# Stage ends by token tile, and five down projections per expert layer in fp32, in a one-core transformer kernel

## What is computed

```python
u = modulate(rmsnorm(h, g_norm_ffn1), sh1, sc1)
h = h + 0.5 * gt1 * swiglu(u, w_ffn1_in, w_ffn1_out)          # "ffn1"
u = modulate(rmsnorm(h, g_norm_mix), sh2, sc2)
h = h + gt2 * token_mixing(u, ...)                            # "mix", ends in @ w_out
u = modulate(rmsnorm(h, g_norm_ffn2), sh3, sc3)
h = h + 0.5 * gt3 * swiglu(u, w_ffn2_in, w_ffn2_out)          # "ffn2"
x = rmsnorm(h, g_final)
for l in range(2):
    ret_o, swa_o, mla_o = ...                                 # from x @ w_in[l]
    mix = concatenate([ret_o, swa_o, mla_o], -1) @ w_out[l]   # "OUT"
    x = layer_norm(ALPHA * x + mix, ln1_g[l], ln1_b[l])
    # 16 experts, 2 per token: h = x @ w_gate_up[e]; a = silu(h[:256]) * h[256:] * gate
    #                          y += a @ w_down[e]
    x = layer_norm(ALPHA * x + grouped_moe(x, ...), ln2_g[l], ln2_b[l])
```

## Time and profile before

| | us |
|---|---|
| time of three runs, median (lowest to highest) | 1220.62 (1219.76 to 1225.07) |
| profiled execution, its own time | 1219.01 |
| its span in the trace | 1217.2 |
| PE, DVE, ACT busy | 1102.7, 898.8, 638.4 |
| read from HBM | 269.41 MB |

### The profile page before, as it was taken

How to read it: one execution, slowest core, us unless ns; L and a number is a source line. 1 busy time by engine, 2 the same in 40 slices (tenths; PEclk the granted TensorE clock), 3 DMA queues, 4 the chain that set the end, 5 groups by cost and what they waited for, 6 DMA issues and landing times.

```text
span 1217.2 us, 24383 instructions
## 1 busy us (share of the span) xinstructions
PE 1102.7 (91%) x10443; PEld 860.7 (71%) x10443; DVE 898.8 (74%) x1107; ACT 638.4 (52%) x770; POOL 88.6 (7%) x104
## 2 busy tenths in 40 slices
PE   5899999899798899999899996989989999698985
PEld 4677777487686477777577774877758777497773
DVE  4799799576657775556557857899985775679996
ACT  1554244433444445444356444777765644477873
POOL 1015421160000100000000000000000000000000
PEclk9799999799899999999989997999989999699998
DMA  9999899345058758665363222599984334169991
GB/s 344 367 360 326 281 351 334 100 157 165 1 182 282 264 189 285 207 207 160 93 221 138 98 81 104 195 381 392 396 270 160 107 104 140 70 209 387 393 391 43
DMA packets 160635, 271.90 MB, mean 223 GB/s; under 512 B 9492, under 2 KB 100216, under 8 KB 160408
## 3 DMA queue, kind: packets, MB, share of 16 engines
q1 hardware_dynamic: 150168, 231.79, 54.9%
q0 software_dynamic: 7904, 29.25, 6.9%
q10 hardware_dynamic: 2464, 9.44, 2.0%
HBM read 269.41 MB, written 1.05 MB: 222 GB/s over the span
## 4 chain that ended last, share of the span: by engine, by line
PE 65%; DVE 22%; DMA 4%; ACT 4%; issue 3%; ACTq 0%; SPq 0%; DVEq 0%
PE ps L703 52%; DVE wlo L457 13%; DMA area<-in_w_ada_dram 2%; ACT whi L432 1%; DMA raw<-in_w_in_dram 1%; DMA raw<-in_exp_w_down_dram 1%; DVE bnst L2011 1%; PE ps L1088 1%; PE ps L1118 1%; DVE hreg L2606 1%; PE ps L1372 1%; PE ps L796 1%; PE ps L1128 1%; PE ps L1348 1%; PE ps L969 1%
## 5 line engine op out<-in xcount | busy, mean ns | idle before, releaser
L457 DVE SCALAR_TENSOR_TENSOR wlo<-raw,whi 128x2048 f16<-128x2048 f32 (+3 forms) x228 | 489.1, 2177 | 45.0 <-ACT whi L432 44.5
L432 ACT ACTIVATE whi<-raw 128x2048 f16<-128x2048 f32 (+3 forms) x228 | 403.7, 1806 | 24.3 <-DMA raw<-in_w_ffn_in_dram 9.9
L703 PE MATMUL ps<-uhi,whi 128*128 128x256 f16 (+2 forms) x1208 | 326.9, 273 | 7.6 <-DVE ulo L2036 4.3
L703 PE MATMUL ps<-ulo,whi 128*128 128x256 f16 (+2 forms) x1208 | 326.6, 273 | 0.0
L703 PE MATMUL ps<-uhi,wlo 128*128 128x256 f16 (+2 forms) x1208 | 326.4, 273 | 0.0
L703 PE MATMUL ps<-whi,hreg 128*128 128x512 f16 (+1 forms) x736 | 232.4, 385 | 15.4 <-DVE area L2590 15.4
L703 PE MATMUL ps<-area,whi 128*128 128x96 f16 (+2 forms) x2168 | 158.4, 212 | 0.1
L703 PEld LDWEIGHTS ps<-area,whi 128*128 128x128 f16 (+2 forms) x2168 | 148.5, 100 | 10.1 <-issue 3.5
L703 PE MATMUL ps<-area,wlo 128*128 128x96 f16 (+2 forms) x1084 | 152.8, 212 | 0.0
L703 PEld LDWEIGHTS ps<-whi,hreg 128*128 128x128 f16 (+1 forms) x736 | 79.7, 108 | 95.5 <-DVE hreg L2611 16.6
L703 PEld LDWEIGHTS ps<-uhi,whi 128*128 128x128 f16 (+1 forms) x1208 | 120.2, 99 | 32.2 <-issue 11.2
(11 more groups left out here) (340 smaller groups left out, 1340.5 us busy)
## 6 DMA issues: line engine op xcount, KB each, us to landing
raw<-in_exp_w_gate_up_dram SPq DMA_DIRECT2D x64, 1024.0 KB, 9.3
raw<-in_w_ffn_in_dram SPq DMA_DIRECT2D x44, 1024.0 KB, 7.2
raw<-in_w_in_dram SPq DMA_DIRECT2D x34, 1024.0 KB, 6.7
raw<-in_exp_w_down_dram SPq DMA_DIRECT2D x32, 1024.0 KB, 10.0
area<-in_w_ada_dram POOLq DMA_DIRECT2D x48, 512.0 KB, 6.7
raw<-in_w_ffn_out_dram SPq DMA_DIRECT2D x22, 1024.0 KB, 7.8
raw<-in_w_out_dram SPq DMA_DIRECT2D x12, 1024.0 KB, 6.0
raw<-in_w_ada_dram ACTq DMA_DIRECT2D x4, 1024.0 KB, 9.4
```

The lines of the kernel that those rows point to most:

```text
L432: act.activation(whi[:, u.slot, 0:n], raw[:, u.slot, 0:n], ACT.Copy, scale=SW)\
L457: dve.scalar_tensor_tensor(out=wlo[:, u.slot, 0:n], in0=raw[:, u.slot, 0:n], scalar=SW, in1=whi[:, u.slot, 0:n], op0=ALU.mult, op1=ALU.sub ...
L703: last = pe.matmul(o, st, mv, start=start and i == 0, stop=stop and i == 2, skip_group_check=True)
```

## The change

The kernel computes the same result. Three things are altered.

1. **Five experts per layer keep their down weights in fp32** (3, 7, 11, 14, 15, `WHOLE`). The 1 MB of each goes into one of two buffers outside the ring (`x_flat`, `gt_flat`, alternating), without `whi` and `wlo`; the activation stays fp32 (`e_whole`), and PE does 4 fp32 matmuls where there were 12 fp16 ones. A layer's experts have 43 ring units instead of 48. Loads of experts 3 and 7 stand in SP's queue ahead of the fifth ring unit, behind four waits; 11 stands behind `("in", 13, 1)`, 14 and 15 behind all ring units of the experts.
2. **gate_up is read as "(p h k)"**, which gives each partition 8 KB in one piece per unit instead of four pieces of 2 KB. The contraction index is permuted by it, so ACT's four copies of `xh` and `xl` per layer read PSUM with a stride of 8 elements.
3. **Stages end by token tile.** The last two down units of ffn1, mix and ffn2 are multiplied tile by tile (`last_downs`: both units for tile 0, then both for tile 1) and announce each half (`yh_done`). `new_x`, the squares, the scaling, the transposes and the split work by tile and half, and the next stage starts with tile 0 (`stage1_by_tokens`, `proj_by_tokens`), with the transposes of tile 1 ahead of the last unit's part for tile 0, also between layer 1 and 2. Ahead of the mixer's first product PE waits for `x_new` 4 and `gt_out` 4. bn_stats of the first half of a tile waits for `yh_done` instead of `y_done`.

The diff, cut:

```diff
+WHOLE = (3, 7, 11, 14, 15)
+MOE_ORDER = [u for c in range(EXPERTS + 2) for u in
+             ([("in", c, 0), ("in", c, 1)] if c < EXPERTS else []) + ([("down", c - 2)] if c - 2 in SPLIT_EXPERTS else [])]
...
-            wi = a["exp_w_gate_up_2"][l].rearrange("e (k p) n -> p e k n", p=P)
+            wi = a["exp_w_gate_up_2"][l].rearrange("e (p h k) n -> p e h (k n)", p=P, h=2)
...
+                for i, src in enumerate(units):
+                    if i == 4:
+                        sp.wait_ge(ret_t, l + 1)
+                        sp.wait_ge(o_made, 6 * (l + 1))
+                        load_whole(WHOLE[0])
+                        sp.wait_ge(ret_o, 4 * (l + 1))
+                        sp.wait_ge(xo_mm, 6 * (l + 1))
+                        load_whole(WHOLE[1])
                     load(Unit(U_L + N_L * l + N_LMIX + i), src)
+                    for c in WHOLE[2:]:
+                        if MOE_ORDER[i] == ("in", c + 2, 1):
+                            load_whole(c)
+                for c in WHOLE[2:]:
+                    if c + 2 >= EXPERTS:
+                        load_whole(c)
...
+            def last_downs(pairs, between=None):
+                for t in range(TT):
+                    for i, (u, th, tl) in enumerate(pairs):
+                        end = i == len(pairs) - 1
+                        for n in range(2):
+                            for f in range(2):
...
+                            if end and n == 0:
+                                last.then_inc(yh_done, 1)
+                        if end:
+                            last.then_inc(y_done, 1)
...
+            token_transposes(0, 0)
+            pe.wait_ge(x_new, 4)
+            pe.wait_ge(gt_out, 4)
+            proj_by_tokens([(Unit(U_MIX + IN1_POS[i]), 256, i) for i in range(3)], 0)
...
+                    if c in WHOLE:
+                        i = WHOLE.index(c)
+                        pe.wait_ge(e_made, EXPERTS * l + c + 1)
+                        pe.wait_ge(whole_in[i % 2], 16 * whole_turn(l, i))
+                        for n in range(2):
+                            for f in range(2):
+                                last = pe.matmul(ps[0:SLOTS, 6 + n, :], e_whole[i % 4][:, f * SLOTS:(f + 1) * SLOTS],
+                                                 whole[i % 2][:, f * D + n * HALF:f * D + (n + 1) * HALF], start=False,
+                                                 stop=c % 4 == 3 and f == 1, skip_group_check=True)
...
-                        act.activation(v[:, t, :], ps[:, 4 + 2 * i + t, :].bitcast(F16), ACT.Copy).then_inc(xt_out, 1)
+                        act.activation(v[:, t, :].rearrange("p (k q) -> p k q", k=KT),
+                                       ps[:, 4 + 2 * i + t, :].bitcast(F16).rearrange("p (q k) -> p k q", k=KT), ACT.Copy).then_inc(xt_out, 1)
...
-            new_x(1)
-            rms_xn(1)
-            norm_split(1)
-            ahead(Unit(U_MIX - 1))
+            for t in range(TT):
+                new_x(0, t)
+                token_scaled(0, t)
+                token_split(0, t, acol[:, 1, :], adacols[:, 8:16])
+                if t == 0:
+                    ahead(Unit(U_MIX - 1))
...
             phase(ffn2)
-            new_x(3)
-            rms_xn(3)
-            norm_split(3)
             ahead(Unit(U_L - 1))
+            for t in range(TT):
+                new_x(2, t)
+                token_scaled(2, t)
+                token_split(2, t, vec8[:, V_GF:V_GF + 8], zero8[:, :])
```

More of the change, by code:

```diff
@@ L62 @@
 OUT_TILES = (1, 2, 0, 3)
-N_L = N_LMIX + 3 * EXPERTS
+WHOLE = (3, 7, 11, 14, 15)
+N_WHOLE = len(WHOLE)
+SPLIT_EXPERTS = [c for c in range(EXPERTS) if c not in WHOLE]
+MOE_ORDER = [u for c in range(EXPERTS + 2) for u in
+             ([("in", c, 0), ("in", c, 1)] if c < EXPERTS else []) + ([("down", c - 2)] if c - 2 in SPLIT_EXPERTS else [])]
+N_L = N_LMIX + len(MOE_ORDER)
 U_END = U_L + LAYERS * N_L
@@ L367, in build @@
         diag_made, last_in = sem("diag_made"), sem("last_in")
+        whole_in, whole_used = [sem(f"whole_in{i}") for i in range(2)], sem("whole_used")
         lt_mm, l_hi, l_lo = sem("lt_mm"), sem("l_hi"), sem("l_lo")
@@ L735, in down @@
                                             False, stop and f == 1, weights_first=False)
+                            if done is not None and n == 0 and f == 1:
+                                last.then_inc(yh_done, 1)
                     if done is not None and t == 0:
@@ L742, in down @@
                     last.then_inc(used, 1)
+            def last_downs(pairs, between=None):
[4 more added lines that the diff above has]
+                            for f in range(2):
+                                w = slice(f * D + n * HALF, f * D + (n + 1) * HALF)
+                                last = split_mm(ps[:, 2 * t + n, :], whi[:, u.slot, w], wlo[:, u.slot, w],
+                                                th[f][:, t * P:(t + 1) * P], tl[f][:, t * P:(t + 1) * P],
+                                                False, end and f == 1, weights_first=False)
+                            if end and n == 0:
+                                last.then_inc(yh_done, 1)
+                        if end:
+                            last.then_inc(y_done, 1)
+                        elif t == TT - 1:
+                            last.then_inc(used, 1)
+                        if t == TT - 1 and not end and between is not None:
+                            between()
+                pe.matmul(ps[0:32, 4, 0:1], zeros16[0:1, 0:32], zeros16[0:1, 0:1], start=True, stop=True,
+                          skip_group_check=True).then_inc(used, 1)
             def hT(par):
@@ L822, in out_part @@
                                         mixlo[:, tile, xs], False, j == 3 and f == 1, weights_first=False)
+                    if j == 3 and n == 0:
+                        last.then_inc(yh_done, 1)
                 return last
@@ L995, in _ @@
             pe.wait_ge(mod_cols, 1)
-            phase(ffn1, {9: gt1_rows, 10: mods2}, before_last=gt2_row, norm=0)
-            pe.wait_ge(gt_out, 4)
-            transposes(1)
+            phase(ffn1, {9: gt1_rows, 10: mods2}, before_last=gt2_row)
             two = [(0, P), (P, P)]
@@ L1050, in out_proj @@
             def out_proj(th, tl):
-                for j in range(4):
+                halves = [[[v[:, 2 * j + f, :] for f in range(2)] for v in (th, tl)] for j in range(4)]
+                for j in range(2):
                     u = Unit(U_MIX + OUT1_POS[j])
                     pe.wait_ge(lo_made, u.count(1))
-                    down(u, [th[:, 2 * j + f, :] for f in range(2)], [tl[:, 2 * j + f, :] for f in range(2)],
-                         stop=j == 3, done=True if j == 3 else None)
-                    if j < 2:
-                        ada_unit(2 + j)
-                pe.matmul(ps[0:32, 4, 0:1], zeros16[0:1, 0:32], zeros16[0:1, 0:1], start=True, stop=True,
-                          skip_group_check=True).then_inc(used, 1)
+                    down(u, *halves[j])
+                    ada_unit(2 + j)
+                u, v = (Unit(U_MIX + OUT1_POS[j]) for j in (2, 3))
+                pe.wait_ge(lo_made, v.count(1))
+                last_downs([(u, *halves[2]), (v, *halves[3])])
             pe.wait_ge(m_lo, 4)
@@ L1062, in _ @@
             pe.wait_ge(mod_cols, 4)
-            transposes(2)
-            phase(ffn2, {10: gt3_rows}, norm=2)
+            token_transposes(1, 0)
+            phase(ffn2, {10: gt3_rows}, q=1)
             pe.wait_ge(gt_out, 6)
-            transposes(3)
+            token_transposes(2, 0)
             for l in range(LAYERS):
@@ L1414, in expert_down @@
-                        down(u, hi, lo, stop=done, done=True if done else None)
+                        down(u, hi, lo)
                     for c in range(EXPERTS):
@@ L1905, in dense @@
                 def dense():
+                    act.wait_ge(pT_mm[l], 1)
+                    for b in range(4):
+                        ins = act.activation((up_hi, up_lo)[b // 2][:, 4 * (b % 2):4 * (b % 2) + 4, :],
+                                             ps[:, b, :].bitcast(F16).rearrange("p (k n) -> p k n", k=4), ACT.Copy)
+                    ins.then_inc(pT_out[l], 1)
                     act.wait_ge(gate_t[l], 1)
@@ L2117, in step @@
                     if last:
-                        ahead(u + 1)
+                        ahead(u + 1, 1 if ph is ffn1 else 2)
                     chunk(ph, c, ph.g0 + c, par)
@@ L2121, in step @@
                     if last:
-                        ahead(u + 2)
+                        if ph is ffn1:
+                            ahead(u + 2)
                     else:
```

391 lines of the change are left out of this document (246 added, 145 removed).

## The result

The changed kernel takes 1210.60 us (median of 5 runs, 1208.76 to 1212.04), the kernel before 1220.19 in the same comparison. The ratio is 0.9919, with a 95% interval from 0.9903 to 0.9935: 9.6 us or 0.8% faster. 1207.8 was forecast. In a second comparison the same kernel gave 1210.54 and 0.9908 [0.9887, 0.9929].

A forecast was written before the change was run, and what follows sets the result against it. PE bounds the kernel on average, DVE the experts. Terms -4.0 - 2.8 + 3.7 - 2.0 - 2.5 - 2.4 - 2.8 = -12.8 from 1219.0 give 1206.2; 1.6 to the median makes 1207.8 us. Own range 1203.5 to 1212 (0.48); 8 in 10: 1199 to 1217.

The forecast's parts named there:

- Experts: Expert layers: five fp32 downs relieve DVE and PE becomes the bound; -4.0 us in layer 1, -2.8 in layer 2.
- half signal: At OUT and behind the experts of both layers: bn_stats runs under PE's second half; 4 x -0.7 = -2.8 us.
- the first wait: Layer 1's experts: PE's wait for the first group's output mostly stays, shrinking from 2.8 to 1.6 us.
- the three signs of being wrong: A growing landing or ACT wait for gate_up, an L1887 copy above 1.3 us, a PE gap before layer 1's last two downs.
- just in time: End of layer 1's experts: layer 2's first weights, queued behind two loads that wait for PE, arrive in time by under 2 us.
- Transfers: Expert weight loads: 8 KB pieces give the few per cent needed; if they bring nothing, an expert layer gives at most 2.6 us.
- that run's rival: Expectation for the 2 KB run: transfers become the bound, 3 to 4 us more in each layer, 1217 to 1219; no chance given.
- End of ffn1: ffn1 to mixer: PE waits for tile 1's `new_x` before its first product; +3.7 us, between +2 and +5.
- Ends of the mixer and ffn2: Next stage starts earlier by tiles: mixer -2.0 us (-1.3 to -2.8), ffn2 -2.5 us (-1.6 to -3.5).
- Layer boundary: Layer 1 to layer 2: PE's gap of 2.6 us for tile 1's split is hidden behind products; -2.4 us.
- The copies of ACT: ACT's strided PSUM reads before the gather: taken as 0; twice the time would be +1.0 us per copy, +8.2 in all.
- the rival that would have made the kernel slower: ACT's strided PSUM read: 1.6 us more per copy cancels the gain, three more gives 1231.8 us; chance 0.07.

## Why the prediction was right

The sign and the size were right: 1207.8 forecast, 1210.6 measured, in the forecast's own range. The terms with a mechanism held; that the total came so near is in part luck, since stretches that the sum put at nothing moved by -2.8, +4.4, +2.8 and -1.7 us and in part cancelled, to +2.7. Step by step:

- **Experts.** Forecast -4.0 and -2.8; the stretches give -4.7 and -3.8 with a half signal of 0.7 in each, so -4.0 and -3.1; the run with the experts alone has the same two numbers. The bound moved from DVE to PE as worked out, the first wait stayed (1.7 where 1.6 was said), and sixteen fp32 records took 6.88 us in the chain, 3.44 for each down as priced. The run with four experts measured the same price from the other side, 0.84. One of the three signs of being wrong did show: a PE gap ahead of layer 1's last down, of 0.7 us. The loads of layer 2 behind those that wait for PE were not "just in time"; the fifth fp32 unit makes SP wait 9.7 us, and with four units gap and wait are gone.
- **Transfers.** The forecast took it that the longer pieces give the few per cent that are needed, and that without them an expert layer gives 2.6 us at most. The run with 2 KB bears both out: there the experts give 1.9 and 1.5 us, with 8 KB 4.0 and 3.0. The price is about half of what that run's rival said, since the ring absorbs part of a DMA rate that is just short. The rate, 395 GB/s at a share of 1.01, again stands above the 358 GB/s that the Trainium skill, "DMA: Bandwidth & Descriptors", section "Where 436 GB/s comes from", gives as the bound of such transfers; this trace and that of the kernel before both disagree with it. "Perfetto Trace Analysis", section "DMA Optimizations", of the Trainium skill says that going from 2 KB to 4 or 8 KB can improve throughput dramatically. Here it turned 6.7 us of ACT's waits into 1.3 and raised the rate in 820 to 851 from 392 to 395 GB/s, worth 3.6 us in the traces and too little to tell in the times.
- **End of ffn1.** +3.7 forecast, +2.8 measured. The mechanism was right: PE waits for tile 1's sum, which stands behind tile 0's split and a weight unit. From the last down to the first product I had 10.7 us (229.66 to 240.4), and it took 10.6; products by tile were to cost 1.5, and take 18.6 us where 17.05 were taken (238.18 to 255.2). Before, 8.5 us lay between the two, so PE starts 2.1 later behind its downs, as forecast, though not later by the clock of the profile, since the downs end earlier. The 0.9 less come ahead of that place, and they are scatter: in the second profile of the changed kernel the whole stretch is +3.8. What I left out is that another order has the gain without the loss: the run with the sum first shows it.
- **Ends of the mixer and ffn2.** -2.0 and -2.5 forecast, -1.6 and -3.0 measured. At the mixer one thing was missed: "tile 1 has long been split" was wrong. Its sum stands in DVE's queue behind tile 0's split, and PE waited 2.4 us in front of tile 1's transposes (414 to 445); the earlier start of tile 0, 3.5 us behind the downs instead of 9.8, paid for it:

```profile
PE ps L882 <- DVE xn L2173: 2.4, 1, 2.4
```

- **Layer boundary.** -2.4 forecast, -1.4 measured. The gap of 2.6 is gone. The clock is 0.61 in 902 to 915 where it was 0.74 before, so part of it went there; that is read from windows and was not tested. In the run with shifted code, where the clock was 0.74, the stretch is 0.6 us shorter.
- **The copies of ACT.** 1.02 us before, 1.02 after; the rival that would have made the kernel slower had no ground.
- **What the sum did not hold.** With the half signals taken out, four stretches in which nothing was to move moved by -2.8, +4.4, +2.8 and -1.7, +2.7 in all. The start is at least in part scatter: it differs by 1.6 us between two executions of the changed kernel. Of the others, +2.0 (layer 1) and -1.0 (layer 2) are stalls of PE's instruction supply that came and went with the place of the code, shown by shifting code that is not executed and by the packets of 16 KB just ahead of their ends. The +4.4 of the attention go with the granted clock, and what is left of the other two, +0.8 and -0.7, is not attributed. Why the clock falls for longer in the attention of the changed kernel, though the work is the same and starts at the same time, stays open.

## What to carry to other kernels

A pipelined stage end is an order in three queues, and the gain lies in that order more than in the split by tiles: the work that releases PSUM for the next stage (here the sum of tile 1) goes ahead of the work that only its own tile needs, and a weight unit between the tiles may be the cover of a wait two steps later, so move one thing at a time. A time that does not move is no proof that an edit costs nothing: compare the stretch it touches, which here repeats to 0.3 us while whole runs scatter by 3. When one engine of two that are nearly equal is relieved, give it no more than brings them level: four fp32 downs beat five, and the fifth also made the queue of loads wait for PE. After a change in code size, look at the stretches that were not changed: a stall of 2 to 6 us behind a branch, with nothing waited for, may be the code's own place.

## What the runs showed of the hardware

- **A stall that depends on where the code lies.** Behind the branch into the expert code PE stands still without a releaser: 2.92 us in the kernel before, 3.17 and again 2.01 (with 8 records between) in the changed one, 6.53 in the one with four experts, 2.99 when code that is not executed moved it. Each of these ends 1.3 to 1.7 us behind a packet of 16 KB on the queue q8 of the kind `instruction`. The records do not name the engine whose code it is; that it is PE's is my inference from this agreement.
- **ACT reads PSUM with a stride of 8 fp16 elements at no cost**: 128x1024 in 1.02 us with and without, eight times each:

```profile
L2036 ACT ACTIVATE area<-ps x8: 1006/1020/1024, 752.8 to 1053.2; 128x1024 f16<-128x1024 f16 x8
```

- **The granted clock differs over identical work**: 0.85 and 0.70 in the same stretch of the kernel before and of the changed one, the latter in both profiles of it; it cost some 3 us there. The other ten runs have 0.70 to 0.72 too.
